# Latent attention: the scores of two heads made together, and each head's probabilities scaled before its head's remaining vector work

## The reference, cut to what matters

```python
q = jnp.concatenate([q[..., :MLA_NOPE], apply_rope(q[..., MLA_NOPE:], cos, sin)], axis=-1)
q = q * ((MLA_NOPE + MLA_ROPE) ** -0.5)
sc = jnp.einsum('bqhd,bkhd->bhqk', q[:, s:e], k[:, :e]).astype(jnp.float32)
sc = jnp.where(mask[None, None], sc, MASK_VALUE)
p = jax.nn.softmax(sc, axis=-1).astype(v.dtype)
outs.append(jnp.einsum('bhqk,bkhd->bqhd', p, v[:, :e]))
```

## Time and profile before

| | |
|---|---|
| median of 3 runs | 1320.78 us |
| lowest, highest | 1319.34, 1324.37 us |
| the profiled execution's own time | 1320.92 us |
| its span | 1319.1 us |
| PE busy, share of the span | 97% |
| DVE, ACT busy | 62%, 46% |
| stage of this change | 518.7 to 575.4 us of the span |

### The profile page before, as it was taken

One profiled execution on the slowest core, in us unless ns is written; L12 is line 12 of the kernel. 1 busy time (PEld: TensorE's weight loads), 2 busy tenths in 40 slices (PEclk: granted clock), 3 DMA queues, 4 the chain that ended last, 5 costly groups with the idle time before them and its releaser, 6 DMA issues. The chain is left out here.

```text
span 1319.1 us, 24384 instructions
## 1 busy us (share of the span) xinstructions
PE 1284.0 (97%) x9407; PEld 1119.2 (85%) x9407; DVE 822.3 (62%) x1495; ACT 608.7 (46%) x1031; POOL 55.1 (4%) x97
## 2 busy tenths in 40 slices
PE   6999999999999999999999999999999999999996
PEld 6999999999999998789999999989999964444444
DVE  7577667588766677466888757858655752222224
ACT  5555555544444555555444446656644531111112
POOL 1000020000000000000000000000000000000000
PEclk9999999999999999999999999999999999999999
DMA  9875456466667544235667776432145659999994
GB/s 389 190 246 179 144 167 214 166 222 223 222 222 237 198 160 135 78 108 193 237 231 236 249 237 232 163 113 93 52 159 187 226 206 398 396 424 426 426 426 161
DMA packets 71189, 295.76 MB, mean 224 GB/s; under 512 B 9718, under 2 KB 10742, under 8 KB 60208
## 3 DMA queue, kind: packets, MB, share of 16 engines
q1 hardware_dynamic: 58896, 257.38, 53.6%
q0 software_dynamic: 12192, 36.95, 9.2%
HBM read 287.76 MB, written 11.53 MB: 227 GB/s over the span
## 5 line engine op out<-in xcount | busy, mean ns | idle before, releaser
L2183 DVE TENSOR_TENSOR ring_low<-ring,w_hi 128x1024 fp32r<-128x1024 f32 x292 | 355.1, 1223 | 171.6 <-ACT w_hi L1694 170.3
L864 PE MATMUL bank<-hn_hi,w_hi 128*128 128x272 f32 (+1 forms) x1416 | 411.3, 290 | 10.8 <-DVE ring_low L2183 10.8
L868 PE MATMUL bank<-hn_hi,ring_low 128*128 128x272 f32 (+1 forms) x1416 | 405.6, 286 | 0.0
L867 PE MATMUL bank<-hn_low,w_hi 128*128 128x272 f32 (+1 forms) x1416 | 404.7, 286 | 0.0
L1694 ACT ACTIVATE w_hi<-ring 128x1024 fp32r<-128x1024 f32 x292 | 302.4, 1051 | 115.5 <-PE bank L864 105.2
L864 PEld LDWEIGHTS bank<-hn_hi,w_hi 128*128 128x128 f32 x1416 | 268.8, 190 | 13.6 <-issue 12.5
L868 PEld LDWEIGHTS bank<-hn_hi,ring_low 128*128 128x128 f32 x1416 | 268.9, 190 | 0.0
L867 PEld LDWEIGHTS bank<-hn_low,w_hi 128*128 128x128 f32 x1416 | 268.5, 190 | 0.3
L864 PE MATMUL bank<-arena_r,w_hi 128*128 128x256 f32 (+1 forms) x784 | 224.7, 287 | 2.3 <-DVE arena L2450 2.2
L868 PE MATMUL bank<-arena_r,ring_low 128*128 128x256 f32 (+1 forms) x784 | 223.1, 285 | 0.0
L867 PE MATMUL bank<-arena_r,w_hi 128*128 128x256 f32 (+1 forms) x784 | 222.7, 284 | 0.0
(11 more groups left out here) (475 smaller groups left out, 1651.3 us busy)
## 6 DMA issues: line engine op xcount, KB each, us to landing
ring<-weights SPq DMA_DIRECT2D x300, 512.0 KB, 3.7
ring<-pairs_in SPq DMA_DIRECT2D x42, 1024.0 KB, 13.1
mod_part<-mod_rows POOLq DMA_DIRECT2D x40, 512.0 KB, 4.6
w_late<-pairs_in SPq DMA_DIRECT2D x14, 1024.0 KB
tab<-pairs_in SPq DMA_DIRECT2D x14, 1024.0 KB
arena<-pairs_in SPq DMA_DIRECT2D x12, 1024.0 KB, 15.3
ring<-pairs_in SPq DMA_DIRECT2D x12, 512.0 KB, 4.5
tab<-tables SPq DMA_DIRECT2D x1, 2858.0 KB, 17.3
```

Source lines behind the costliest of these rows:

```text
L864: begun = mm(dst[:, 0:cols], wh, high(k), start=k == 0, stop=False)
L867: mm(dst[:, 0:cols], wh, low(k), start=False, stop=False)
L868: last = mm(dst[:, 0:cols], wl, high(k), start=False, stop=k == K - 1)
L2183: tt_(ring_lo[:, slot, :], ring[:, slot, :], w_hi[:, n % SPLITS, :], ALU.subtract).then_inc(S("w_lo_ready"), 1)
```

## The change

TensorE makes the scores of two heads in one go. `mla_scores(first)` takes an even head and the odd one behind it. For a query block it issues the two products over 128 rows, then the two over 64 rows, into banks 4 and 5. The pairs stand at other places than the single scores did: heads 0 and 1 right behind head(1), and heads 2 and 3, 4 and 5, 6 and 7 behind the turns 1, 3 and 5. Before its first product a pair waits for the copies of the keys and queries of both heads, and for the probabilities of the head before the pair.

VectorE's loop is reordered. Head i's probabilities come in step i, directly behind its front, so VectorE waits there for ScalarE's exponentials of the same head. The low half of the output of head i-3 stands ahead of the front instead of behind it. The low halves of the weights for head i+3 come last in both.

```diff
--- before.py
+++ after.py
@@ -1168,20 +1168,23 @@
                 kv_tile()
                 q_tile()
 
-            def mla_score(i, dst):
-                if i == 0:
+            def mla_scores(first):
+                pair = [(i, bank[4 + i % 2], slice(64 * (i % 2), 64 * (i % 2) + ROPE)) for i in (first, first + 1)]
+                if first == 0:
                     pe.wait_ge(S("q_roped"), 5)
-                wait_stored(pe, at["kn", i])
-                wait_stored(pe, at["qn", i])
-                if i >= 2:
-                    pe.wait_ge(S("head_p"), i - 1)
-                r = 64 * (i % 2)
+                else:
+                    pe.wait_ge(S("head_p"), first)
+                for i, _, _ in pair:
+                    wait_stored(pe, at["kn", i])
+                    wait_stored(pe, at["qn", i])
                 for lo, hi, q0 in [(0, META + P, 0), (META + P, MLA_W, P)]:
                     w = hi - lo
-                    mm(dst[:, lo:hi], q_m[:, i, q0:q0 + P], k_m[:, i, 0:w], start=True, stop=False)
-                    last = mm(dst[:, lo:hi], qrope[r:r + ROPE, i // 2, q0:q0 + P], krope[r:r + ROPE, 0, 0:w],
-                              start=False, stop=True)
-                return last
+                    for i, dst, _ in pair:
+                        mm(dst[:, lo:hi], q_m[:, i, q0:q0 + P], k_m[:, i, 0:w], start=True, stop=False)
+                    for i, dst, r in pair:
+                        last = mm(dst[:, lo:hi], qrope[r, i // 2, q0:q0 + P], krope[r, 0, 0:w], start=False, stop=True)
+                        if hi == MLA_W:
+                            last.then_inc(S("mla_scored"), 1)
 
             def turn(tag, j, pv, meta):
 
@@ -1223,19 +1226,18 @@
                 values("mla", j, slice(j * P, (j + 1) * P), True, slice(0, P))
 
             head(0)
-            for i in range(2):
-                head(2 * i + 1)
-                mla_score(i, bank[4 + i % 2]).then_inc(S("mla_scored"), 1)
-                if i == 0:
-                    head(2)
+            head(1)
+            mla_scores(0)
+            head(2)
+            head(3)
             for j in range(MH + 1):
                 if j < MH:
                     pe.wait_ge(S("head_p"), j + 1)
                     if j:
                         pe.wait_ge(S("mla_pt"), j)
                     turn("mla", j, p_m[:, j % 2, :], True)
-                if j + 2 < MH:
-                    mla_score(j + 2, bank[4 + j % 2]).then_inc(S("mla_scored"), 1)
+                if j % 2 and j + 2 < MH:
+                    mla_scores(j + 1)
                 if j:
                     mla_values(j - 1)
                 if j + 4 < MH:
@@ -2494,16 +2496,18 @@
                 dve.wait_ge(S("om_hi_ready"), j + 1)
                 tt_(o_m_lo[:, j, :], src[:, 0:SEQ], o_m_hi[:, j, :], ALU.subtract).then_inc(free, 1)
 
+            def mla_probs(j):
+                dve.wait_ge(S("head_exp"), j + 1)
+                s = stats[:, 8 * j:8 * j + 8]
+                link(nc.vector.reciprocal(s[:, 6:8], s[:, 4:6]))
+                for n, (lo, hi) in enumerate([(0, META + P), (META + P, MLA_W)]):
+                    a = p_m[:, j % 2, lo:hi]
+                    last = ts_(a, a, s[:, 6 + n:7 + n], None, ALU.mult)
+                last.then_inc(S("head_p"), 1)
+
             for i in range(MH + 3):
-                if 1 <= i <= MH:
-                    j = i - 1
-                    dve.wait_ge(S("head_exp"), i)
-                    s = stats[:, 8 * j:8 * j + 8]
-                    link(nc.vector.reciprocal(s[:, 6:8], s[:, 4:6]))
-                    for n, (lo, hi) in enumerate([(0, META + P), (META + P, MLA_W)]):
-                        a = p_m[:, j % 2, lo:hi]
-                        last = ts_(a, a, s[:, 6 + n:7 + n], None, ALU.mult)
-                    last.then_inc(S("head_p"), 1)
+                if 3 <= i:
+                    o_m_low(i - 3)
                 if i < MH:
                     dve.wait_ge(S("mla_scored"), i + 1)
                     if i >= 2:
@@ -2515,8 +2519,8 @@
                         last = nc.vector.tensor_reduce(s[:, j:j + 1], p_m[:, i % 2, lo:hi], AX, ALU.max)
                     link(last)
                     ts_(s[:, 2:4], s[:, 0:2], -1.0, None, ALU.mult).then_inc(S("head_max"), 1)
-                if 3 <= i:
-                    o_m_low(i - 3)
+                if i < MH:
+                    mla_probs(i)
                 if i + 3 < MH:
                     lows(at["qn", i + 3])
             add_and_split(at["wo1"], SEQ, lambda k: h[:, k, XC], "ffn1", "ffn1", lambda k: hn_hi[:, k, XC],
```

## The result

| | before | after |
|---|---|---|
| median of 11 runs each | 1320.35 us | 1327.51 us |
| lowest, highest | 1317.14, 1325.18 | 1325.20, 1333.81 |
| the profiled execution | 1320.92 (span 1319.1) | 1333.81 (span 1332.0) |
| mean granted clock of the profiled execution | 0.995 | 0.982 |

The ratio of after to before is 1.0057, interval [1.0042, 1.0072]. The change makes the kernel 7.2 us slower. The forecast was 1323.0 us, no change. The measured 1327.5 lies 0.5 us above the range and 0.1 above 1327.4, from which the prediction would have called the kernel slower (chance 0.10). Nearest to what happened is the third rival, the clock at half from turn 5 on, priced at 1328.0 us; in the profile the clock comes back for 3.4 us in between.

The account below looks back on a forecast made before the run. TensorE was taken to set the stage's length. Pairs at -5.4 us and waits of 0.65, 2.0, 1.8 and 1.6 gave +0.65; a clock fall of 1.5 made +2.2, from 1320.8 to 1323.0 us, full range 1318.5 to 1327.0.

Parts of the forecast that it names:

- third rival: Clock stays at half from turn 5 into the projection: +7.2 us with the full-clock sum, 1328.0 us, chance 0.09.
- The pair: On TensorE, two heads' scores together take 2.82 us against 4.18 singly; four pairs save 5.4 us.
- The rival of a failed overlap: In pairs, the second head's 64-row passes queue: +2.8 or +1.4 us, 1325.8 or 1324.4 us, chance 0.12, half each.
- The wait of the first pair: Behind head(1), TensorE waits for ScalarE's copy of head 1's query: 0.65 us added.
- Turns 0 to 4: The first two turns' waits, 0.78 us together, keep their size; none to speak of ahead of turns 2 to 4.
- Turn 5: TensorE waits 2.0 us ahead of turn 5: VectorE and ScalarE need 9.3 us, TensorE has 7.26 us of work.
- Turn 6: TensorE waits 1.8 us ahead of turn 6, where there was no wait before.
- Turn 7: TensorE waits 1.8 us ahead of turn 7 against 0.20 before, 1.6 us more; turns 6 and 7 are 3.9 apart.
- The sum at full clock: Over the stage, the pairs' saving and the added waits come to +0.65 us before any fall of the clock.
- the clock's term: One fall to half clock in the tail, between 562 and 579 us, for some 3.4 us: 1.5 us added.
- the longer case: Half clock from turn 5 into the projection: about +2.5, +2.3 and +1.7 us for its three parts, chance 0.09.

Follow-up runs that it names:

- again: The changed kernel, unedited, measured once more on another chip: 1328.50 us, ratio 1.0058.
- filled: The changed kernel with four extra matmuls that nobody reads ahead of each of turns 5, 6 and 7: 1321.20 us, ratio 1.0006.
- single_tail: The changed kernel with the scores of heads 6 and 7 made singly at their old places, behind turns 4 and 5: 1322.61 us, ratio 1.0019.
- dve_alone: The kernel before with only VectorE's new order, TensorE's program and single scores as before: 1327.81 us, ratio 1.0059.
- best: The changed kernel with heads 6 and 7 scored singly at old places, output's low half behind the probabilities, first pair behind head(2): 1321.01 us, ratio 1.0003.
- serial: The changed kernel with pairs at their new places but each head's four score products behind one another: 1328.65 us, ratio 1.0064.
- dve_filled: The kernel before with VectorE's new order and four extra matmuls that nobody reads ahead of turn 7: 1320.51 us, ratio 1.0001.
- single_olow: The changed kernel with heads 6 and 7 scored singly at old places and the output's low half behind the probabilities: 1323.08 us, ratio 1.0026.
- pe_alone: The changed kernel with VectorE's order as before, so only TensorE's pairs are new: 1335.85 us, ratio 1.0122.
- best2: The changed kernel with first pair behind head(2), heads 6 and 7 scored singly at old places, VectorE's old order from head 5: 1313.37 us, ratio 0.9968.

## Why the prediction was wrong, by its steps

- **The pair**, 2.82 us: right, 2.80. The rival of a failed overlap is excluded. A window of 0.02 us in the timeline after (535.94 to 535.96) has the first rotary passes of both heads in it, x2 in one group:

```profile
535.73 0.29 PE L1183 MATMUL bank<-arena 128*128 128x144 f32 x1
535.95 0.39 PE L1185 MATMUL bank<-arena 64*128 64x144 f32 x2
```

- **The wait of the first pair**, 0.65: right, 0.56, put down to ScalarE's copy:

```profile
519.42 0.73 PE L1183 MATMUL bank<-arena 128*128 128x144 f32 x4 [0.56 <-ACT arena L1889]
```

- **Turns 0 to 4**: I left their waits at the same size. Turns 0 and 1 wait 0.23 and 0.21 us instead of 0.31 and 0.47, turns 2 to 4 not at all. Right but for 0.3.
- **Turn 5**, 2.0: right, 2.12. **Turn 6**, 1.8: right, 1.79 (1.93 in `again`). **Turn 7**, 1.8: right at full clock (turns 6 and 7 are 3.85 us apart in after, in `again` and in `filled`, 3.9 was forecast), though at half clock TensorE itself fills most of it: 0.30 in after, 1.74 in `again`.
- **The sum at full clock**, +0.65: right. In after the sixteenth projection matmul behind the first is at 585.43, in before at 577.47, 7.96 later. Turn 5 and pair at half clock are 0.53 and 2.40 of it (1.13 against 0.60, 5.20 against 2.80), turn 7 0.52, values 6 and 7 2.45 (576.55 to 581.85, against 572.60 to 575.45), the projection 1.56 (3.58 against 2.02). That is 7.46; 0.50 is left. In `filled`, all at full clock, `wo1` starts 0.86 later, and 0.33 of that is there already at the first matmul of head(1)'s query (516.77 against 516.44).
- **The step that failed** is the size of the clock's term, in the prediction's words: "So I expect one fall. It costs 0.49 of 3.5 us, 1.7 us, if all of it lies in work that TensorE sets, and less where it lies in a wait; I take 1.5." The waits that I had worked out gave two stretches at half clock, 20.5 us instead of 3.5, and 7.5 us instead of 1.5. The error was to take the length of one stretch from the earlier trace rows as that of any, and to count one fall for three waits. In the earlier trace rows dense work follows the wait; here transposes, short products and the next wait do. That this difference makes the stretch longer is argued and not shown: `single_tail` and `dve_alone` have the same work behind a wait of 2.12 us ahead of turn 7, and 10.3 and 6.9 us at half clock. The prediction had the sum for the longer case, +2.5, +2.3 and +1.7; measured are 2.9, 3.0 and 1.6. It gave that case 0.09.

The point is sharpest in `filled` against after and `again`: the same waits, filled or idle, and 6 to 7 us between the times.

One thing stays open. The stretches at half clock between 980 and 1025 us in after's profile are there in part in `best`, `serial` and `dve_filled`, and not in `again`, `filled`, `single_tail`, `single_olow`, `dve_alone`, `pe_alone` or `best2`. `again` is the same program as after, so no edit explains them, and what brings them was not tried. They may be a part of the scatter between executions. In `best2` five executions take 1312.64 to 1313.37 us at a mean granted clock of 0.995 to 0.997 and two take 1319.43 and 1321.00 at 0.990, and no profile of those two shows where.

## What to carry to other kernels

Before you save matmul time in a stretch without dense work, work out the interval from scores to probabilities and what TensorE has between; if a wait of about 2 us appears among short products, price it as that wait plus a stretch at double length that takes in everything up to the next dense work and 3 to 6 us of the dense work too. Here the half clock cost 3.5 to 7.5 us and not 1.5. If the wait can't be avoided, a few products without a reader inside it bring most of that back. And use an order of the other engines for each stretch that fits it: the order that helps while dense work stands between heads lost time in the tail, and `best2`, with both orders, beat either kernel.

## What the runs showed of the hardware

- The stretches at half clock that began in or behind waits of 1.7 to 2.3 us lasted between 3.4 and 13.7 us. They were short where dense matmuls followed (3.4 us in `best`, from 557.5) and longer where transposes and value products followed (6.9 us in `dve_alone`, 10.3 in `single_tail`, 13.7 in after). The same program had 6.8 us in one execution and 3.4 in the other for the first fall.
- The clock came back only 3.2 to 6.1 us into the dense matmuls of `wo1`: 3.65 us in after, 5.3 in `again` (580.54 to 585.8), 5.7 in `single_tail`, 3.9 in `dve_alone`, 3.2 in `serial` and 6.1 in `pe_alone`.
- A wait doesn't always bring it down: that of 2.11 us at 545.61 in `best` didn't (PEclk 1.00 from 547.0 to 557.5), that of 2.26 us at 556.54 did, though dense matmuls of a head follow both. In `single_olow`, with the same two waits, both did. In `filled`, eight matmul passes (1.99 us) in place of each of the three waits kept it at 1.00 in the profiled execution.
- At half clock a full pair takes 1.86 times as long (5.20 us against 2.80), a turn 1.88 times (1.13 against 0.60).
- Products over 64 rows from the two halves of the rows start within 0.02 us of each other even when they add to banks that 128-row products just wrote. By the Trainium skill, page "TensorEngine Tiling (Array Packing)", section "Key Properties", a change of tiling mode drains TensorE. The rows show no drain as such, and they agree that fewer changes take less time. In `serial` there are seven changes between 128 and 64 rows inside a pair instead of three, and the pair takes 1.48 us more: 1.09 for the second head's 64-row groups, which no longer lie beside the first one's (0.44 and 0.65), and 0.39 for 128-row products that no longer stand together.
